# Gated recurrence of four heads: decays by products of gates instead of logs and exps, the four heads in one block

## Reference: what is computed

```python
f = lb + (1.0 - lb) * sigmoid(fc)
# per head, chunk of tokens:  gc = log f, kc = 1 - f
b = cumsum(gc, axis=2)
a = einsum('bhnmd,bhnd->bhnm', exp(b_n - b_m) * kc, qc)        # m <= n only
o = einsum('bhnm,bhmv->bhnv', a, vc) + einsum('bhnd,bhdv->bhnv', qc * exp(b), S)
S = exp(b_last) * S + einsum('bhmd,bhmv->bhdv', kc * exp(b_last - b), vc)
```

## Time and profile before

| | us |
|---|---|
| median of 3 runs (lowest, highest) | 3437.83 (3436.85, 3438.65) |
| the profiled execution: its time | 3438.71 |
| its span in the trace | 3436.9 |
| busy: PE, PEld, DVE, ACT, POOL | 3103.2, 2949.1, 1617.8, 573.4, 1166.3 |
| mean granted TensorE clock | 0.926 of full speed |

### The profile page before, as it was taken

The page is one execution under the profiler, slowest core; times in us unless marked ns, Lnnn a source line. Parts: engine busy times, 40 slices in busy tenths (PEclk is TensorE's granted clock), DMA queues, the critical chain, the costliest instruction groups (busy, mean ns, idle before and its releaser), DMA issues. The chain is left out here.

```text
span 3436.9 us, 44160 instructions
## 1 busy us (share of the span) xinstructions
PE 3103.2 (90%) x18135; PEld 2949.1 (86%) x18135; DVE 1617.8 (47%) x1798; ACT 573.4 (17%) x914; POOL 1166.3 (34%) x609
## 2 busy tenths in 40 slices
PE   7988678899999999998977787689888999999999
PEld 6987468789999999998976676459868999999999
DVE  4152454347626345254146635664445644626443
ACT  3111122242000000002122222251243000000000
POOL 3332033123334344333346533203203434434342
PEclk9999689999999999999975688799999999999999
DMA  3101131401111111113100021003131111111112
GB/s 118 47 26 37 24 95 55 141 25 49 40 49 43 43 49 37 49 36 109 37 7 14 23 76 37 14 1 113 50 129 46 45 41 49 39 49 47 37 49 79
DMA packets 274511, 176.43 MB, mean 51 GB/s; under 512 B 15134, under 2 KB 261278, under 8 KB 274398
## 3 DMA queue, kind: packets, MB, share of 16 engines
q1 hardware_dynamic: 274398, 174.84, 16.8%
HBM read 158.56 MB, written 16.27 MB: 51 GB/s over the span
## 5 line engine op out<-in xcount | busy, mean ns | idle before, releaser
L327 PE MATMUL psum<-moving_hi,w_hi 128*128 128x384 f32 (+1 forms) x3888 | 1283.5, 330 | 70.4 <-PEq L515 24.7
L329 PE MATMUL psum<-moving_hi,w_lo 128*128 128x384 f32 (+1 forms) x3888 | 1277.4, 329 | 0.0
L328 PE MATMUL psum<-moving_lo,w_hi 128*128 128x384 f32 (+1 forms) x3888 | 1277.1, 328 | 0.0
L289 POOL TENSOR_TENSOR w_hi<-w_raw,one 128x1024 fp32r<-128x1024 f32 (+2 forms) x236 | 406.6, 1723 | 1934.7 <-PE psum L329 1387.9
L327 PEld LDWEIGHTS psum<-moving_hi,w_hi 128*128 128x128 f32 x3888 | 738.0, 190 | 78.7 <-issue 60.9
L328 PEld LDWEIGHTS psum<-moving_lo,w_hi 128*128 128x128 f32 x3888 | 738.2, 190 | 0.5 <-issue 0.5
L329 PEld LDWEIGHTS psum<-moving_hi,w_lo 128*128 128x128 f32 x3888 | 737.4, 190 | 0.0
L294 POOL TENSOR_TENSOR w_lo<-w_raw,w_hi 128x1024 fp32r<-128x1024 f32 (+2 forms) x236 | 575.1, 2437 | 18.5
L368 DVE TENSOR_TENSOR residual<-psum,residual 128x768 f32 x192 | 130.1, 719 | 490.7 <-PE psum L329 490.1
L327 PE MATMUL psum<-hidden_hi,w_hi 128*128 128x384 f32 (+1 forms) x1056 | 344.6, 326 | 3.2 <-DVE hidden_lo L1896 3.2
L329 PE MATMUL psum<-hidden_hi,w_lo 128*128 128x384 f32 (+1 forms) x1056 | 345.1, 327 | 0.0
(11 more groups left out here) (308 smaller groups left out, 3085.5 us busy)
## 6 DMA issues: line engine op xcount, KB each, us to landing
w_raw<-in_ffn_w_gate SPq DMA_DIRECT2D x44, 512.0 KB, 3.8
w_raw<-in_ffn_w_up SPq DMA_DIRECT2D x44, 512.0 KB, 3.8
w_raw<-in_ffn_w_down SPq DMA_DIRECT2D x48, 384.0 KB, 3.1
w_raw<-in_od_w_in SPq DMA_DIRECT2D x22, 512.0 KB, 3.8
w_raw<-in_ev_w_in SPq DMA_DIRECT2D x20, 512.0 KB, 3.7
w_raw<-in_mem_w_kv SPq DMA_DIRECT2D x16, 512.0 KB, 3.6
work_h<-in_cache_mem_kT SPq DMA_DIRECT2D x4, 2048.0 KB, 12.0
work_h<-in_cache_mem_v SPq DMA_DIRECT2D x4, 2048.0 KB, 16.9
```

The lines of the kernel that those rows point to most:

```text
L289: nc.gpsimd.tensor_tensor(hi, raw, ONE.to_broadcast([P, kt * P]), ALU.mult).then_inc(own.sem, 1)
L327: pe.matmul(out, sh, mh, start=(k == 0), stop=False)
L328: pe.matmul(out, sh, ml, start=False, stop=False)
L329: return pe.matmul(out, sl, mh, start=False, stop=(k == kt - 1))
```

## The change

1. The two small blocks are gone. Two thirds of the gains are loaded at the end of the feed-forward block, the other tables by the first projection (`loads=tables`, at the end of SP's list), without `RESET`. The lower bound is made on DVE and ScalarE inside the second projection (`meanwhile`).
2. The logs, the running sum, the offsets and all exps of the recurrence are gone. GpSimd makes a tree of gate products (`grow`): for every pair of neighbours of the level below one product, 544 then 272, 136, 64, 32, 16 and 8 wide.
3. Keys and queries are scaled in place, level by level (`enter`, `update`). At level lv the right queries have been multiplied by the product since the middle, and the left keys by the product up to the middle, so after level 7 they carry the whole decay of the inter part. So `update(lv)` must wait for `score(lv)`, which reads the old values, and `score(lv + 1)` must wait for `update(lv)`.
4. The masked score is written to the score tile by `copy_predicated` (DVE, PSUM to SBUF where the mask is not zero) instead of a product with the mask and an addition on GpSimd. The two score tiles are cleared once at the start.
5. All heads are in one block. TensorE's list puts a piece of head h - 1's inter part ahead of each score of head h. The gate and key are made by ScalarE (`prepare`), and `VBD` by GpSimd (`spread`). `sample_states` is 8 instructions of 128x128 instead of one product and two additions.

The diff, cut to its core:

```diff
 def feed_forward, sync:
+                    if l == 0 and o == steps()[-1][2]:
+                        sp.dma_start(g.GAIN[:, 0:2 * KT], io["gain1"][:, 0:2 * KT]).then_inc(g.loaded.sem, 16)
 def _layer1:
-    run(g.load, [(g.GAIN[:, :], io["gain1"]), ... (RESET, io["hgrn_reset"]), ... (ONE_HOT, io["onehot"])])
-    run(lower_bound)
+    run(g.project, ws[2][0], ..., lead=Lead(...), loads=tables)
+    run(g.project, ws[0][0], ..., meanwhile=Meanwhile([lower_peak, lower_share], lower_exp))
 tensor:
+                def score(h, lv):
+                    pe.wait_ge(updated.sem, updated.at(8 * h + lv))
+                    pe.wait_ge(masked.sem, masked.at(8 * h + max(1, lv - 1)))
...
+                inter = [turn_keys, keys_values, sample_outputs, sample_keys_values, lambda i: outputs(i, range(0, 3)),
+                         lambda i: outputs(i, range(3, 6)), lambda i: outputs(i, range(6, 8))]
+                for h in range(HEADS + 1):
+                    if h < HEADS:
+                        score_diagonal(h)
+                    for lv in range(1, LEVELS + 1):
+                        if h:
+                            inter[lv - 1](h - 1)
+                        if h < HEADS:
+                            score(h, lv)
 vector:
-    forget(); sum_logs(); rests(); decay_operands(); pair(lv); mask(lv)
+                def enter(h):
+                    dve.wait_ge(scored.sem, scored.at(8 * h + 1))
+                    dve.tensor_tensor(query(h), query(h), F, ALU.mult).then_inc(updated.sem, 1)
+                def update(h, lv):
+                    dve.wait_ge(scored.sem, scored.at(8 * h + lv + 1))
...
+                    dve.tensor_tensor(q, q, ends[:, :, 0:1].to_broadcast([P, n // w, w // 2]), ALU.mult)
+                    dve.tensor_tensor(k, k, ends[:, :, 1:2].to_broadcast([P, n // w, w // 2]), ALU.mult).then_inc(updated.sem, 1)
+                def mask(h, lv):
...
+                    last = dve.copy_predicated(A[...][:, :, :, w // 2:], m.unsqueeze(1).to_broadcast([P, NBLK, P // w, w // 2]), PS[:, lv % 2, :]...)
+                for h in range(HEADS + 1):
+                    if h < HEADS:
+                        enter(h)
+                        mask_diagonal(h)
+                    for lv in range(1, LEVELS + 1):
+                        if h < HEADS:
+                            update(h, lv)
+                            mask(h, lv)
+                        if h and lv == 2:
+                            chain_states(h - 1)
+                        if h and lv == 4:
+                            sample_states(h - 1)
 scalar:
+                    act.activation(F, key(h), ACT.Identity, scale=COL[:, 16 + h:17 + h], bias=COL[:, 20 + h:21 + h]).then_inc(forgot.sem, 1)
...
+                    act.activation(key(h), F, ACT.Identity, scale=-1.0, bias=g.ONE[:, 0:1]).then_inc(keyed.sem, 1)
 gpsimd:
-    offsets(lv), add(lv)
+                def grow(h):
+                    for lv in range(1, LEVELS + 1):
...
+                        last = nc.gpsimd.tensor_tensor(decays(h, lv), pairs[:, :, 0], pairs[:, :, 1], ALU.mult)
+                for A in SCORES:
+                    nc.gpsimd.memset(A, 0.0).then_inc(cleared.sem, 1)
+                grow(0)
+                for h in range(HEADS):
+                    spread(h)
+                    if h + 1 < HEADS:
+                        grow(h + 1)
 sync, for each head i: load S0, store the last chain state, [i == 3: the next projection's two weight loads], store S0, wait for both
```

More of the change, by code:

```diff
@@ L1979, in _layer1 @@
     INV = SPARE[:, 1, :]
     ws = [g.columns(w_in[:, 512 * i:512 * (i + 1)], KT, 4) for i in range(5)]
-    run(g.project, ws[2][0], HHL, KT, 4, To(OT, times=INV, rows=IC), then=ws[0], lead=Lead([X[:, k, :] for k in range(KT)], gain=0, inv=INV, spill=True, summed=True))
-    run(g.project, ws[0][0], HHL, KT, 4, To(R, 0, func=ACT.Silu, times=INV), then=ws[1])
+    run(g.project, ws[2][0], HHL, KT, 4, To(OT, times=INV, rows=IC), then=ws[0], lead=Lead([X[:, k, :] for k in range(KT)], gain=0, inv=INV, spill=True, summed=True), loads=tables)
@@ L1983, in _layer1 @@
+    run(g.project, ws[0][0], HHL, KT, 4, To(R, 0, func=ACT.Silu, times=INV), then=ws[1], meanwhile=Meanwhile([lower_peak, lower_share], lower_exp))
     run(g.project, ws[1][0], HHL, KT, 4, To(R, 4, func=ACT.Sigmoid, times=INV))
+    for c in (peaked, exped):
+        c.adds(1)
     CHAIN, S0 = view(g.Wf, 3 * T, NBLK, P), view(g.Wf, 3 * T + 1024, NB, P)
-    E = [g.Wf[:, i * T:(i + 1) * T] for i in range(3)]
+    F, TREE = g.Wf[:, 0:T], [g.Wf[:, (1 + i) * T:(2 + i) * T] for i in range(2)]
     KTS = g.Wf[:, 2048 + 3 * T:2048 + 3 * T + P]
@@ L2087, in chain_states @@
                         else:
[L2088 removed]
+                            last = dve.scalar_tensor_tensor(CHAIN[:, j, :], CHAIN[:, j - 1, :], ENDS[:, i, j:j + 1], ps, ALU.mult, ALU.add)
                         last.then_inc(chained.sem, 1)
[L2090 to L2100 removed]
@@ L2101, in _ @@
-                if intra:
-                    forget()
-                    sum_logs()
-                if inter:
-                    rests()
-                if intra:
-                    mask_diagonal()
-                    pair(1)
-                if inter:
-                    decay_operands()
-                if intra:
-                    pair(2)
-                    mask(1)
-                    pair(3)
-                    mask(2)
-                if inter:
-                    chain_states()
@@ L2118, in _, with sample_states @@
-                if intra:
-                    pair(4)
-                    mask(3)
-                    pair(5)
-                    mask(4)
-                if inter:
-                    sample_states()
-                if intra:
-                    pair(6)
-                    mask(5)
-                    pair(7)
-                    mask(6)
-                    mask(7)
+                        dve.wait_ge(chained.sem, chained.at(NBLK * i + j + 1))
+                def sample_states(i):
+                    dve.wait_ge(kv.sem, kv.at(2 * i + 2))
+                    for b in range(NB):
+                        last = dve.scalar_tensor_tensor(S0[:, b, :], S0[:, b, :], ENDS[:, i, NBLK + b:NBLK + b + 1],
+                                                        PSf[:, 6 * 512 + b * P:6 * 512 + (b + 1) * P], ALU.mult, ALU.add)
+                    last.then_inc(s_in.sem, 1)
@@ L2284, in hgrn, with take_output @@
-            if inter:
-                @block.sync
-                def _(sp):
-                    sp.dma_start(S0, io["state_hgrn"].rearrange("b h k v -> h k b v")[i]).then_inc(g.loaded.sem, 16)
-                    if not intra:
+                def take_output(i):
+                    act.wait_ge(o_ready.sem, o_ready.at(i + 1))
+                    act.activation(OT[:, i, 0:SEQ], PSf[:, 4 * 512:4 * 512 + SEQ], ACT.Copy).then_inc(o_out.sem, 1)
+                prepare(0)
+                for h in range(HEADS + 1):
+                    if h:
+                        take_keys(h - 1)
+                    if h + 1 < HEADS:
+                        prepare(h + 1)
+                    if h:
+                        take_sample_output(h - 1)
+                        take_output(h - 1)
@@ new lines, in _ @@
+            @block.sync
+            def _(sp):
+                for i in range(HEADS):
+                    if i:
+                        sp.wait_ge(o_sample.sem, o_sample.at(i))
+                    sp.dma_start(S0, io["state_hgrn"].rearrange("b h k v -> h k b v")[i]).then_inc(s_loaded.sem, 16)
+                    sp.wait_ge(chained.sem, chained.at(NBLK * i + NBLK))
+                    g.store(sp, io["hgrn_state_prompt"][i], CHAIN[:, NBLK - 1, :])
+                    if i == HEADS - 1:
+                        sp.wait_ge(updated.sem, updated.at(8 * HEADS))
```

402 lines of the change are left out of this document (157 added, 245 removed).

## The result

The change makes the kernel faster by 1.8%, a little over twice what I forecast. The median of 4 runs is 3378.23 us (3372.38 to 3380.08), against 3438.06 us (3436.85 to 3438.65, 4 runs) before: ratio 0.9824 with a 95% interval of 0.9807 to 0.9841. That is 59.8 us less, where the forecast was 3411 and its range ended at 3390. The profiled execution took 3380.08 us with a span of 3378.3. Its mean granted clock is 0.935 (0.926 before).

A forecast was written before the change was run, and what follows sets the result against it. The recurrence was taken as a chain through four engines, none full, mostly with TensorE at 1.2 GHz. Terms -8.5 + 5.1 - 17.6 - 5.8 = -26.8 us gave 3411 us, range 3390 to 3427.

The forecast's parts named there:

- setup: Two small blocks before the projection: removing them leaves one boundary of 8.9 us lost there, saving 8.5 us.
- head 0: First head of the recurrence, with no earlier head's work to hide updates: 48.5 against 43.4 us, 5.1 slower.
- the tail: End of the recurrence after the last head: transposes start earlier on already scaled keys, 21.2 against 27.0 us, 5.8 saved.
- The rival that the tables come late or the boundary stays: Setup: removing the two small blocks gives nothing, total 3419.5 us; no separate chance given.
- the 48.6 us called TensorE's own work: Heads 1 to 3: TensorE's claimed own work within each head's 53.5 us sum.
- my 2.1 and 2.8: Heads 1 to 3: 2.1 us for update 7 and mask 7; 2.8 for `enter`, `mask_diagonal` and two hand-overs.
- The bound on the predicated copy: Masks: copy priced like the product, about 0.7 us per 512 columns; half from below, scan's 2.23 ns a column from above.
- The rival of the dear copy: Masks: predicated copy at the reciprocal's rate, 6.4 ns a column, costs 38 us more, total 3449 us; chance 0.05.
- the 0.5 us a head that I gave this: Heads 1 and 2: update 4 slowed by GpSimd's `grow` beside it, 1 us in two heads, averaged to 0.5.
- the term of the sum that corrects for TensorE's clock in heads 1 to 3: Heads 1 to 3: the outputs' clock rise is lost; one short rise a head counted, 1.5 us back.
- the 53.5 us of the sum at 1.2 GHz: Heads 1 to 3: length of one head with TensorE's pieces priced at 1.2 GHz, before corrections to 52.5 us.
- The clock rises and stays: Heads 1 to 3: higher TensorE clock holds, 33 us a head, total 3351 us, half effect 3381; chance 0.08.

The follow-up runs named there:

- the setup's run: Kernel before with only the two small blocks removed (tables loaded by the first projection, lower bound inside the second), recurrence untouched: 3429.94 us, ratio 0.9973.
- the idle products in head 0: Kernel after plus four unread 128-column identity products in each of six pauses between head 0's scores: 3363.91 us, ratio 0.9783.
- the split diagonal: Kernel after with the first four blocks of the next head's diagonal no longer waiting for mask 7, only the other five: 3369.70 us, ratio 0.9802.
- outputs in one run: Kernel after with a head's 15 output products in one run ahead of score 5 instead of three groups: 3392.69 us, ratio 0.9869.

## Why the prediction was wrong in size

**Right.** The direction, and most terms: setup -8.5 (8.4 in the trace, 8.5 by itself); head 0 slower, +3.8 for +5.1; the tail -7.9 for -5.8. The rival that the tables come late or the boundary stays fell with the setup's run. What bounds the recurrence was read rightly too: the chain of score and update sets the pace. One reading was loose: the 48.6 us called TensorE's own work leave out the turned keys (2.2), so less of a head was waiting than it says. The prices hold where the clock is low (scores 4.01 and 3.67, sample keys times values 3.78), and the new waits are where I put them. The wait view of the kernel after, TensorE over the recurrence (total us, times, longest):

```profile
PE psum L2049 <- DVE work_r L2119: 9.9, 9, 1.5
...
PE psum L2049 <- DVE residual L2129: 7.3, 4, 3.3
PE psum L2040 <- DVE residual L2135: 6.3, 3, 2.1
```

2.1 a head at mask 7 and 0.7 to 1.7 at the diagonal's mask (3.3 in head 0), for my 2.1 and 2.8, of which the turned keys cover part. The update waits are head 0's and the last of each head.

**The bound on the predicated copy.** VectorE by form over the recurrence of the kernel after (busy us, mean ns):

```profile
L2119 DVE TENSOR_TENSOR work_r<-work_r,work_w 128x512 f32<-128x512 f32 x16 | 11.4, 712 | 0.0
...
L2135 DVE COPY_PREDICATED residual<-constants,psum 128x512 f32<-128x512 uint32 x28 | 24.5, 873 | 0.0
```

The mean of 873 ns mixes two prices, as VectorE's timeline in head 1 shows:

```profile
1805.66 0.73 DVE L2118 TENSOR_TENSOR work_r<-work_r,work_w 128x544 f32<-128x544 f32 x1 [3.74 <-PE psum L2049]
...
1812.69 1.28 DVE L2135 COPY_PREDICATED residual<-constants,psum 128x512 f32<-128x512 uint32 x1
...
1819.51 0.69 DVE L2135 COPY_PREDICATED residual<-constants,psum 128x512 f32<-128x512 uint32 x1
```

0.69 to 0.73 at levels 3 to 7, my value, and 1.28 to 1.30 at levels 1 and 2, where the copied columns stand alone or in pairs. The dear ones end under the next piece, so they cost nothing, and mask 7, on the path, is at the cheap price. The rival of the dear copy fell. The product of level 1, whose operands step two words, takes 0.73. The rule on single words with gaps between them (the Trainium skill, Vector Engine (DVE) Microarchitecture Reference, section 5.2) is not borne out for it. It goes in the direction of what the copy does at level 1, but by it pairs of words would run at the full rate, and at level 2 the copy is as slow as at level 1. GpSimd's small products of the tree had no row before: 1.09 us for the largest to 0.20 for the smallest, and none is waited for. The second product of update 4 in head 2, which met GpSimd's tree, took 0.90 us instead of 0.69: the 0.5 us a head that I gave this was more than it needed.

**The step that failed** is the term of the sum that corrects for TensorE's clock in heads 1 to 3: "The change cuts that run in three short ones, so that gift goes" and "I count one short rise a head, 1.5 us back". The heads measured 7.8, 9.4 and 16 us below the 53.5 us of the sum at 1.2 GHz. The outputs cut in three lift the clock as the whole run did (0.65 for 0.64 in head 1), and taking outputs out costs 22.9 us though it saves work; behind the keys times values it rises too. The rise comes two or three times a head, and four scores of head 2 ran with it. I had the mechanism as a rival, "The clock rises and stays", with 3381 us at half of its effect. The measured 3378 is near that, but the clock didn't stay: it rose and fell. The rival had a chance of 0.08, because two runs of 64-column scores had stayed at 1.2 GHz. That argument was half of one: such scores by themselves did not lift the clock, but once something else had lifted it they ran at it for a while, two of them behind the whole run of outputs (1.90 and 2.00) before it fell (3.67). By the Trainium skill (TensorE: Matmul & The Clock Gate, What's actually happening) activity lifts the throttle. The denser stream here agrees with that in direction, and the two runs of scores still do not agree with it as it stands.

**What stays open.** Why one stream of instructions takes 37.5 us in one execution and 45.7 in another is known only as far as the pattern above goes, the clock's last fall 4.1 or 3.7 us ahead of `enter`. The Trainium skill (same page and section) has the chip decide on a rhythm of its own, which does not start with the kernel; the pattern would fit that, but no run here tests it. Nor is it known why the sample keys times values (64 rows, 512 columns, 3.78 us) took the lower clock in heads 1 to 3 and why four idle products behind them didn't lift it. Nor why 1.5 us are given back between L360 and the recurrence; the kernel with the setup alone does the same (165.8 us), so it belongs to the setup.

The best versions are the kernel after with the idle products in head 0, 3363.91 us with no delay and 3361.15 with 2.2 us of delay (ratio 0.978), and the split diagonal, 3369.70, which does no idle work and gained about 8 us with both delays tried.

## What to carry to other kernels

Price each piece of a chain on TensorE at both clock levels, find in the trace which pieces a rise follows, and give what stands behind such a piece the higher price; that one kind of piece never lifted the clock by itself is no evidence that it runs low behind another. Dense work of one part put between the latency-bound steps of another covers their waits (two thirds of the gain of heads 1 to 3 here) and speeds up the steps themselves (one third), and short groups did as well as one long run. Taking work out and finding the time unchanged or longer is the cleanest sign of it. Small variants are compared with several delays, since one alone was off by 7 us here.

## What the runs showed of the hardware that was not expected

- 64-column fp32 products without a pause stayed at 1.2 GHz for 13.9 us when they began there. Behind a run of outputs two groups of them, with pauses of 1.4 us, took 1.90 and 2.00 us at the higher clock, and the third 3.67 at the lower (outputs in one run, head 1).
- The same head, instruction for instruction, took 45.67 us and 37.53 us, at a granted clock of 0.65 and 0.82, with the clock's last fall 3.7 and 4.1 us ahead of its `enter`.
- A predicated copy of 512 columns from PSUM takes 0.69 to 0.73 us when the copied columns stand in runs of four or more, and 1.28 to 1.30 us when they stand alone or in pairs; a two-input product with a step of two words takes 0.73 us for 544 columns, no more than a dense one (0.69 for 512).
